# Eight combining sums a layer given to accumulating DMA, and two rows of a LayerNorm moved behind the last weight chunks

## The reference

```python
def conv_ffn(x, w_up, conv_w, conv_b, w_down):
    up = x @ w_up
    a, g = up[..., :D_FF], up[..., D_FF:]
    g = causal_dwconv(g, conv_w) + conv_b
    return (jax.nn.gelu(g) * a) @ w_down

for layer in range(2):                      # alpha = sqrt(2)
    x = layer_norm(alpha * x + mix, ...)
    x = layer_norm(alpha * x + cross_attend(x, mem, ...), ...)
    x = layer_norm(alpha * x + conv_ffn(x, ...), ln_ffn_g[layer], ln_ffn_b[layer])
...
def second_block(x, c, ...):
    h = rms_norm(x, norm_g) * (1.0 + scale) + shift
    proj = h @ w_in
    ...
```

## Time and profile before

| what | value |
|---|---|
| runs of the kernel before | 1760.81, 1761.2, 1763.09 us |
| profiled execution | 1760.65 us |
| its span in the trace | 1758.8 us |
| TensorE busy | 98% of the span |
| VectorE, ScalarE, GpSimd busy | 63%, 39%, 10% of the span |

### The profile page before, as it was taken

The page is one execution under the profiler, slowest core; times in us unless marked ns, Lnnn a source line. Parts: engine busy times, 40 slices in busy tenths (PEclk is TensorE's granted clock), DMA queues, the critical chain, the costliest instruction groups (busy, mean ns, idle before and its releaser), DMA issues.

```text
span 1758.8 us, 27808 instructions
## 1 busy us (share of the span) xinstructions
PE 1728.8 (98%) x11461; PEld 1447.6 (82%) x11461; DVE 1110.8 (63%) x1624; ACT 684.7 (39%) x1045; POOL 184.4 (10%) x246
## 2 busy tenths in 40 slices
PE   8999999999999999999999999999998999999998
PEld 7888988988888879888998888888886767777766
DVE  5567266454568795454726755567988585566784
ACT  5332352232235643213235232223554543345452
POOL 4202001200011112000210200001112000011000
PEclk9999999999999999999999999999999999999999
DMA  9882912973345858833492265455683422112412
GB/s 301 259 217 99 252 39 79 279 230 110 126 138 186 260 166 204 247 97 118 114 283 77 83 204 156 143 183 185 201 277 108 153 65 81 34 43 62 169 37 84
DMA packets 175453, 270.44 MB, mean 154 GB/s; under 512 B 10488, under 2 KB 97780, under 8 KB 174560
## 3 DMA queue, kind: packets, MB, share of 16 engines
q1 hardware_dynamic: 147488, 189.90, 34.2%
q0 software_dynamic: 26368, 73.51, 15.7%
q10 hardware_dynamic: 1472, 5.26, 0.8%
HBM read 253.67 MB, written 61.09 MB: 179 GB/s over the span
## 4 chain that ended last, share of the span: by engine, by line
PE 88%; DVE 7%; issue 2%; ACT 1%; DMA 1%; POOL 1%; SPq 0%; ACTq 0%; DVEq 0%
PE ps L365 26%; PE ps L367 26%; PE ps L366 26%; DVE WL L342 2%; PE ps L1007 2%; PE ps L554 1%; PE ps L2575 1%; PE ps L2595 1%; PE ps L2589 1%; DMA RAW<-ffn_w_down 1%; PE ps L1981 0%; DVE SM L1637 0%; PE ps L2609 0%; DVE LATE L2656 0%; PE ps L2712 0%
## 5 line engine op out<-in xcount | busy, mean ns | idle before, releaser
L342 DVE TENSOR_TENSOR WL<-RAW,WH 128x1024 fp32r<-128x1024 f32 x325 | 393.3, 1222 | 387.7 <-ACT WH L332 387.2
L332 ACT ACTIVATE WH<-RAW 128x1024 fp32r<-128x1024 f32 x325 | 341.0, 1058 | 559.8 <-PE ps L367 450.6
L365 PE MATMUL ps<-XH,WH 128*128 128x512 f32 (+1 forms) x1416 | 524.6, 370 | 2.6 <-DVE WL L342 1.5
L367 PE MATMUL ps<-XH,WL 128*128 128x512 f32 (+1 forms) x1416 | 518.1, 366 | 0.0
L366 PE MATMUL ps<-XL,WH 128*128 128x512 f32 (+1 forms) x1416 | 517.9, 366 | 0.0
L365 PEld LDWEIGHTS ps<-XH,WH 128*128 128x128 f32 x1416 | 267.4, 189 | 50.1 <-issue 5.3
L367 PEld LDWEIGHTS ps<-XH,WL 128*128 128x128 f32 x1416 | 267.3, 189 | 43.3
L366 PEld LDWEIGHTS ps<-XL,WH 128*128 128x128 f32 x1416 | 267.5, 189 | 40.7
L365 PE MATMUL ps<-WH,XH 128*128 128x512 f32 x696 | 279.1, 401 | 7.9 <-DVE WL L342 7.0
L367 PE MATMUL ps<-WH,XL 128*128 128x512 f32 x696 | 271.9, 391 | 0.0
L366 PE MATMUL ps<-WL,XH 128*128 128x512 f32 x696 | 271.6, 390 | 0.0
(11 more groups left out here) (404 smaller groups left out, 2063.7 us busy)
## 6 DMA issues: line engine op xcount, KB each, us to landing
RAW<-ffn_w_up SPq DMA_DIRECT2D x176, 256.0 KB, 3.5
weight_sums<-ffn_w_down POOLq DMA_DIRECT2D x12, 1536.0 KB, 18.5
RAW<-w_in SPq DMA_DIRECT2D x33, 512.0 KB, 3.9
RAW<-xa_wkv SPq DMA_DIRECT2D x32, 512.0 KB, 7.5
RAW<-weight_sums SPq DMA_DIRECT2D x32, 512.0 KB, 4.6
weight_sums<-ffn_w_down POOLq DMA_DIRECT2D x12, 1280.0 KB, 31.1
RAW<-c_w_in SPq DMA_DIRECT2D x24, 512.0 KB, 7.2
LATE<-w_ada SPq DMA_DIRECT2D x24, 512.0 KB, 5.2
```

The lines of the kernel that those rows point to most:

```text
L332: e.activation(halves_of(i)[0][:, :, 0:w], raw(i)[:, :, 0:w], ACT.Copy).then_inc(*w_hi.up(i))
L342: e.tensor_tensor(wl[:, :, 0:w], raw(i)[:, :, 0:w], wh[:, :, 0:w].bitcast(F), ALU.subtract).then_inc(*w_lo.up(i))
L365: e.matmul(o, lh, rh, start=start, stop=False)
L367: return e.matmul(o, ll, rh, start=False, stop=stop)
```

## The change

Two things change. First, the eight additions of alpha x with U or Y, a layer, leave VectorE: in the up product, ScalarE scales each of the four rows of XR by alpha in place (`residual_act`, after the column blocks 2 to 5), and GpSimd's queue then adds U (to x11), the sum U + P6 (to x21) and Y (to x12 and x22) by eight accumulating DMAs of 128x512 (`combined_pool`), issued behind the token loads. The sum U + P6 gets a place of its own (`sum_place`). VectorE adds P7 to x21 at s = 26 and subtracts it from x22 at s = 27, now with waits for the DMAs. Second, the order of the LayerNorm's rows: in the first layer rows 0 and 1 stay between the last chunks, in the second they go behind all forty, where each row's end stands between the next row's statistics and its gathering.

```diff
+    def residual_act(e, l, turned, t):
+        for q in range(2):
+            e.wait_ge(*turn.at((turned, t, q)))
+        e.activation(XR[:, t, :], XR[:, t, :], ACT.Copy, scale=ALPHA).then_inc(*ffn_a.up(("residual", l, t)))
...
+    def combined_pool(e, l):
+        n = ("ffn", l)
+
+        def added(name, t, j, src):
+            e.wait_ge(*ffn_a.at(("residual", l, t)))
+            e.dma_start(XR[:, t, 512 * j:512 * j + 512], src, accum_op=ALU.add).then_inc(*comb[name].up((l, t)))
+        for u in range(2):
+            e.wait_ge(*dn_a.at(("u", l, u)))
+            added("x11", u, 0, U[u])
+        for u in range(2):
+            e.wait_ge(*ln_v.at((n, "sum", u)))
+            added("x21", 2 + u, 0, sum_place(l, u))
+        for u in range(2):
+            e.wait_ge(*ln_v.at((n, "y", u)))
+            added("x12", u, 1, Y[u])
+        for u in range(2):
+            added("x22", 2 + u, 1, Y[u])
...
-                if s == 20:
+                if s == 21:
                     e.wait_ge(*dn_a.at(("u", l, u)))
-                    scaled(u, 0, U[u]).then_inc(*ln_v.up((n, "x11", u)))
-                if s == 21:
                     e.wait_ge(*gemm.at(("down", l, 6, u)))
...
-                if s == 23:
-                    e.wait_ge(*ln_v.at((n, "y", u)))
-                    scaled(u, 1, Y[u]).then_inc(*ln_v.up((n, "x12", u)))
-                if s == 24:
+                if s == 26:
                     e.wait_ge(*gemm.at(("down", l, 7, u)))
-                    scaled(2 + u, 0, ps.tile(("down", l, 7, u))[:, :]).then_inc(*ln_v.up((n, "ax21", u)))
-                if s == 25:
-                    scaled(2 + u, 1, Y[u]).then_inc(*ln_v.up((n, "ax22", u)))
-                if s == 26:
-                    e.wait_ge(*ln_v.at((n, "ax22", u)))
+                    e.wait_ge(*comb["x21"].at((l, 3)))
+                    e.tensor_tensor(x(2 + u, 0), x(2 + u, 0), ps.tile(("down", l, 7, u))[:, :], ALU.add).then_inc(
+                        *ln_v.up((n, "x21", u)))
+                if s == 27:
+                    e.wait_ge(*comb["x22"].at((l, 3)))
...
-            if s == 30:
-                row(0)
-            if s == 31:
-                row_end(0)
-            if s == 32:
-                row(1)
-            if s == 33:
-                row_end(1)
+            if l == 0 and s in (30, 32):
+                row((s - 30) // 2)
+                row_g((s - 30) // 2)
+            if l == 0 and s in (31, 33):
+                row_end((s - 31) // 2)
...
-            for t in range(2, 4):
+            for t in range(4):
                 row(t)
-                if t == 3:
-                    bias_dve(e, 2)
-                row_end(t)
+                if t:
+                    row_end(t - 1)
+                row_g(t)
+            bias_dve(e, 2)
+            row_end(3)
             bias_dve(e, 3)
...
                     tokens_pool(e, l)
                     down_pool(e, l)
+                    combined_pool(e, l)
                 if (name, l) == ("ffn", 1):
                     early_pool(e)
```

More of the change, by code:

```diff
@@ L318, in programs @@
     dn_a = sig("dn_a", "A")
+    comb = {name: sig(f"comb_{name}", "dma", 16) for name in ("x11", "x12", "x21", "x22")}
     made = {"hi": 0, "lo": 0, "w": 0}
@@ L1272, in up_act @@
                 gelu_act(e, l, nb, i)
+            if 2 <= nb < 6:
+                residual_act(e, l, turned, nb - 2)
         hi_to(e, first["up", l, 10] + 3 + NH)
@@ L1352, in programs, with sum_place @@
     Y = [SCR[:, 512 * u:512 * u + 512] for u in range(2)]
+    def sum_place(l, u):
+        return late(512 + 512 * u, 512) if l == 0 else late(4096 + 1024 * u, 512)
+    def combined_pool(e, l):
[14 more added lines that the diff above has]
+            added("x22", 2 + u, 1, Y[u])
     def token_place(l):
@@ L1667, in down_dve @@
             for u in range(2):
-                if s == 20:
+                if s == 21:
                     e.wait_ge(*dn_a.at(("u", l, u)))
-                    scaled(u, 0, U[u]).then_inc(*ln_v.up((n, "x11", u)))
-                if s == 21:
                     e.wait_ge(*gemm.at(("down", l, 6, u)))
-                    e.wait_ge(*ln_v.at((n, "x11", u)))
-                    e.tensor_tensor(U[u], U[u], ps.tile(("down", l, 6, u))[:, :], ALU.add).then_inc(
+                    if l:
+                        e.wait_ge(*tok_out.at((l, 10)))
+                    e.tensor_tensor(sum_place(l, u), U[u], ps.tile(("down", l, 6, u))[:, :], ALU.add).then_inc(
                         *ps.empties(("down", l, 6, u), ln_v, (n, "sum", u)))
@@ L1678, in down_dve @@
                     e.wait_ge(*gemm.at(("down", l, 5, u)))
-                    e.tensor_tensor(Y[u], ps.tile(("down", l, 5, u))[:, :], U[u], ALU.subtract).then_inc(
+                    e.tensor_tensor(Y[u], ps.tile(("down", l, 5, u))[:, :], sum_place(l, u), ALU.subtract).then_inc(
                         *ps.empties(("down", l, 5, u), ln_v, (n, "y", u)))
-                if s == 23:
-                    e.wait_ge(*ln_v.at((n, "y", u)))
-                    scaled(u, 1, Y[u]).then_inc(*ln_v.up((n, "x12", u)))
-                if s == 24:
+                if s == 26:
                     e.wait_ge(*gemm.at(("down", l, 7, u)))
-                    scaled(2 + u, 0, ps.tile(("down", l, 7, u))[:, :]).then_inc(*ln_v.up((n, "ax21", u)))
-                if s == 25:
-                    scaled(2 + u, 1, Y[u]).then_inc(*ln_v.up((n, "ax22", u)))
-                if s == 26:
-                    e.wait_ge(*ln_v.at((n, "ax22", u)))
+                    e.wait_ge(*comb["x21"].at((l, 3)))
[3 more added lines that the diff above has]
+                    e.wait_ge(*comb["x22"].at((l, 3)))
                     e.tensor_tensor(x(2 + u, 1), x(2 + u, 1), ps.tile(("down", l, 7, u))[:, :], ALU.subtract).then_inc(
                         *ps.empties(("down", l, 7, u), ln_v, (n, "x22", u)))
-                if s == 27:
-                    e.wait_ge(*ln_v.at((n, "ax21", u)))
-                    e.tensor_tensor(x(2 + u, 0), x(2 + u, 0), U[u], ALU.add).then_inc(*ln_v.up((n, "x21", u)))
                 if s == 28:
                     e.wait_ge(*gemm.at(("down", l, 2, u)))
+                    e.wait_ge(*comb["x11"].at((l, 1)))
                     add(2, u, 0)
@@ L1734, in down_dve @@
         row(2)
+        row_g(2)
         turn_dve(e, n, 1)
@@ L1738, in down_dve @@
         row(3)
+        row_g(3)
         lo_to(e, i0 + 38 + NH)
```

7 lines of the change are left out of this document (3 added, 4 removed).

## The result

The changed kernel takes 1768.44 us (median of 8 runs, 1766.54 to 1770.22) against 1762.2 us before (8 runs, 1760.81 to 1763.09): ratio 1.0037, 95% interval 1.0029 to 1.0046. It is slower by some 6 us, above the forecast of 1760.5 and above the range's upper end of 1764.8. The profiled execution took 1768.84, its span is 1766.8, 8.0 longer than before.

The account below looks back on a forecast made before the run. TensorE, busy 98% of the span, was taken as the bound, so only its waits could yield time. Terms 0 + 0 - 0.7 against 1760.65 gave 1759.95, or 1760.5 us on the median's scale; range 1757.0 to 1764.8.

Parts of the forecast that it names:

- The eight sums taken from VectorE: VectorE, first layer's down product: 5.5 us a layer taken off becomes idle time, TensorE's 2.2 us of waits stay; gain 0.
- ScalarE's scalings, and the four later loads behind the transfers: Up product's scalings, 4.2 us a layer, and second layer's loads about 4.3 us behind transfers on GpSimd's queue: cost 0.
- so it lands at 625.3 with 6 us to spare: cost 0: Last x22 transfer, first layer: issued by 620.7, landing after 4.6 us, wanted by 631.35, so VectorE loses nothing.
- VectorE's list behind 629.61: First layer's down product: VectorE's chain from the subtraction at 629.61 to 654.15 keeps its start and length, without slack.
- The late-transfer rival: First layer's step 27 waits for late transfers, paid one for one: 1763.7 us at 13.9, 1770.8 at 21.0; chance 0.15.
- The rows behind the last chunk: Second layer's end: TensorE gains 3.7 us of weight waits, gives back 2.9 to 3.0 through serial row ends; -0.7.
- TensorE's new pause: Rival, behind second layer's bias matmuls: about 4 us pause slows transposes; 1763.6 us, or 1766.2 for all 47; chance 0.12.

## Why the prediction failed, step by step

**The eight sums taken from VectorE: 0.** Right. VectorE is still paced by ScalarE's roundings up to the pair of step 27, and the freed time is idle.

**ScalarE's scalings, and the four later loads behind the transfers: 0.** The scalings took 1.04 each. Nothing speaks against the step: no wait of TensorE in the up product, and the bias matmuls waited for no load.

**The transfers: "so it lands at 625.3 with 6 us to spare: cost 0".** This is the step that failed. It asked when the transfers land, and not whom they hold up meanwhile: the weight loads beside them were put at nothing without a reason. But the issues took 0.85 to 1.89 each, not 0.54, the DMA engines were full for 16 us, the loads landed after 6.9 instead of 3.7, and two of them kept ScalarE waiting for 2.6 and 2.3 us. VectorE's list behind 629.61 has no slack, as the prediction itself says; it then let only the transfers, and not the loads, be late there. In the first layer that cost 1.85 by the waits and 2.15 by the half clock in the profiled execution, 3.3 by the runs. In the second it cost the new wait of 1.3.

The landing was wrong as well. Transfers landed after 5.3 to 13.1, median 7.3, where 4.6 was taken. VectorE's pair for x22 waited for one until 633.68, which is 1.6 behind the 631.35 at which it was wanted, with the lag of 0.77 taken off. That this added nothing is luck: the second late load would have held VectorE until 635.14 in any case, 0.2 longer than the transfer did.

**The late-transfer rival** (chance 0.15) had the place right, and the price one for one as far as the waits go; the half clock behind them came on top. Its transfers were late, but the loads, which it does not name, were later.

**The rows behind the last chunk: weight waits gone, given back by the serial loop, -0.7.** The mechanism was right. Without transfers the waits on weights are gone; the loop took 4.57 to 4.60 where 4.44 was taken and 5.01 bounded it. The step on GpSimd took 0.22 once VectorE's instruction with two SBUF inputs no longer ran beside it; beside that instruction, for row 0, it still took 1.31 at 1350.29. The Trainium skill, "SBUF — State Buffer", section "Who interferes with whom", says that a VectorE instruction with two SBUF inputs contends with a GpSimd instruction that reads SBUF. The trace agrees (1.31 against 0.22). With TensorE kept busy the rows' move won 0.3 in the profile, and came out at 0.9997 by the runs, whose interval takes in no change.

**TensorE's new pause** (chance 0.12) came as described: 4.94 us against some 4, and half clock behind it, in every trace with the pause left empty. Its size was off: 1.5 in the traces with transfers and 0.8 in those without, not 3.1, because most of the slow transposes lie ahead of the last row's scaling, which TensorE would have waited for anyway. The Trainium skill, "TensorE: Matmul & The Clock Gate", section "HAM oscillation — how this bites in real kernels", describes a kernel whose pauses between bursts drop the array to half rate. The trace agrees, with a granted clock of 0.50 behind the pause.

**The range** took each rival alone. Late weights and a slow clock came together, and the one brought the other on: behind a longer wait of TensorE the clock fell in the first layer, too, which no rival had. In the profile 4.0 are lost in the first layer's down product. From the matmul at 918.90 to the end of the transposes another 2.8 are lost (5.20 to 8.04), about what the late loads (1.3 to 1.5) and the clock (1.5) make, less the 0.3 that the rows win.

What stays open: why the clock falls behind some waits of TensorE of about 2 us (2.33 in the first layer of the changed kernel, 1.87 in the second with the rows inside) and not behind others (2.29 with the pause filled, 2.2 in the kernel before). The changed kernel's own runs differ in this: the mean granted clock is 0.995 or 0.996 in seven of the eight, and 0.998 in the shortest, 1766.54.

## What to carry to other kernels

Price a transfer twice: when it lands, and what it takes from the loads that run beside it, above all where an engine behind those loads has no slack. Work taken from an engine that is paced by another is worth nothing until the place where that engine itself is late; there, moving one row behind the last urgent subtraction was worth more than eight sums saved earlier. When waits of TensorE are moved together into one pause, look at its clock behind the pause, and put other work or a smaller pause there.

## What the runs showed of the hardware

- Accumulating transfers of 256 KB between SBUF tiles landed after 5.3 to 13.1 us (median 7.3) and took GpSimd 0.85 to 1.89 to issue; the same transfers as plain copies 3.9 to 7.3 (median 5.0) and 0.54. With the DMA engines full, 244 to 296 GB/s went through beside the accumulating ones, 354 to 367 beside the plain ones.
- The eight adding transfers of a layer raised the landing of 512 KB weight loads beside them from 3.7 to 6.9 us (medians), eight copies to 5.5, four adding transfers to 4.9. Only the first kept ScalarE waiting for the two loads named above.
- TensorE's granted clock went to 0.50 behind pauses of 4.9 and 2.8 us, and also behind waits of 2.33 and 1.87, but not behind others of 2.29 and 2.2. With 40 more transposes in the pause of 4.9 it stayed at 1.00.
